# Cross attention scheduled by couples of heads instead of by single units

## The reference, cut to what matters

```python
def cross_attention(h, mem, g_mem, w_cq, w_ckv, w_co):
    q = (h @ w_cq).reshape(n, S, N_HEADS_X, HEAD_DIM_X)        # 4 heads of 128
    k, v = jnp.split(rms_norm(mem, g_mem) @ w_ckv, 2, axis=-1) # 256 memory rows per stream
    s = jnp.einsum('nqhd,nmhd->nhqm', q, k).astype(jnp.float32) * (HEAD_DIM_X ** -0.5)
    p = jax.nn.softmax(s, axis=-1)
    o = jnp.einsum('nhqm,nmhd->nqhd', p, v.astype(jnp.float32)).reshape(n, S, D_X).astype(h.dtype)
    return o @ w_co
```

## Time and profile before

| | |
|---|---|
| median of 3 runs | 2303.09 us (2302.89 to 2307.04) |
| profiled execution, its time | 2302.74 us |
| profiled execution, its span | 2301.0 us |
| PE busy | 2201.2 us, 96% |
| DVE / ACT / POOL busy | 49% / 27% / 34% |
| mean granted TensorE clock | 0.983 |

### The profile page before, as it was taken

How to read it: one execution, slowest core, us unless ns; L and a number is a source line. 1 busy time by engine, 2 the same in 40 slices (tenths; PEclk the granted TensorE clock), 3 DMA queues, 4 the chain that set the end, 5 groups by cost and what they waited for, 6 DMA issues and landing times. The chain is left out here.

```text
span 2301.0 us, 39032 instructions
## 1 busy us (share of the span) xinstructions
PE 2201.2 (96%) x13528; PEld 1931.4 (84%) x13528; DVE 1116.0 (49%) x2157; ACT 627.4 (27%) x1556; POOL 783.1 (34%) x436
## 2 busy tenths in 40 slices
PE   7999999999999999999999999899999999999996
PEld 7988977987788888888798889789878888888885
DVE  3575655537554145235355746554465532551453
ACT  3455454234311011001044554433342110110011
POOL 3311112441344444444331111035323444444442
PEclk9999989999999999999999999899999999999998
DMA  5100121221121121211141001122111221111122
GB/s 216 69 20 22 36 74 39 93 73 37 47 64 64 64 64 64 64 60 58 66 147 38 20 29 38 65 83 74 56 37 56 64 64 62 57 64 64 64 65 82
DMA packets 40286, 145.11 MB, mean 63 GB/s; under 512 B 4688, under 2 KB 4944, under 8 KB 39888
## 3 DMA queue, kind: packets, MB, share of 16 engines
q1 hardware_dynamic: 32832, 117.45, 15.6%
q10 hardware_dynamic: 7312, 25.78, 3.1%
HBM read 133.78 MB, written 9.44 MB: 62 GB/s over the span
## 5 line engine op out<-in xcount | busy, mean ns | idle before, releaser
L742 POOL CAST w_hi<-w_landed_tile 128x1024 fp32r<-128x1024 f32 x216 | 225.1, 1042 | 1469.5 <-PE ps L783 1459.2
L783 PE MATMUL ps<-x_turned,w_hi 128*128 128x512 f32 (+1 forms) x3072 | 666.8, 339 | 3.9 <-DVEq L1352 2.1
L783 PEld LDWEIGHTS ps<-x_turned,w_hi 128*128 128x128 f32 x3072 | 523.1, 188 | 107.5 <-issue 4.3
L744 POOL TENSOR_TENSOR w_lo<-w_landed_tile,w_hi 128x1024 fp32r<-128x1024 f32 x216 | 557.8, 2582 | 17.3
L783 PE MATMUL ps<-w_hi,x_turned 128*128 128x256 f32 (+1 forms) x2304 | 549.4, 321 | 8.1 <-ACT scratch L1209 4.9
L783 PEld LDWEIGHTS ps<-w_hi,x_turned 128*128 128x128 f32 x2304 | 392.6, 194 | 33.0 <-ACT scratch L1209 6.1
L783 PE MATMUL ps<-x_turned,w_lo 128*128 128x512 f32 (+1 forms) x1536 | 394.4, 338 | 0.0
L783 PE MATMUL ps<-w_hi,regions 128*128 128x512 f32 (+1 forms) x1312 | 374.8, 369 | 0.0
L783 PE MATMUL ps<-w_lo,x_turned 128*128 128x256 f32 (+1 forms) x1152 | 360.1, 313 | 0.0
L783 PEld LDWEIGHTS ps<-w_hi,regions 128*128 128x128 f32 x1312 | 238.7, 188 | 42.1 <-DVE x_residual L1465 0.6
L1259 ACT ACTIVATE scratch<-scratch 128x768 f32<-128x768 f32 x44 | 37.3, 848 | 840.3 <-DVE scratch L1522 840.3
(11 more groups left out here) (90 smaller groups left out, 2074.5 us busy)
## 6 DMA issues: line engine op xcount, KB each, us to landing
w_landed_tile<-weights_dram SPq DMA_DIRECT2D x216, 512.0 KB, 3.5
x_hbm<-x_residual ACTq DMA_DIRECT2D x2, 3072.0 KB, 15.3
x_residual<-x_hbm ACTq DMA_DIRECT2D x4, 1536.0 KB, 8.3
rows<-mem_in_dram ACTq DMA_DIRECT2D x8, 512.0 KB, 4.3
scratch<-mem_in_dram ACTq DMA_DIRECT2D x8, 512.0 KB, 5.9
x_residual<-x_in_dram SPq DMA_DIRECT2D x6, 512.0 KB, 5.9
out<-scratch ACTq DMA_DIRECT2D x6, 512.0 KB, 2.7
gain<-gains_dram ACTq DMA_DIRECT2D x3, 512.0 KB, 16.0
```

What stands on the lines that cost most here:

```text
L742: nc.gpsimd.tensor_copy(W_HI[:, s, :], W_IN[:, s, :]).then_inc(w_rounded, 1)
L744: nc.gpsimd.tensor_tensor(W_LO[:, s, :], W_IN[:, s, :], W_HI[:, s, :].bitcast(F32), ALU.subtract).then_inc(w_split, 1)
L783: ins = pe.matmul(dst, lhsT, rhs, start=start, stop=stop, skip_group_check=True)
```

## The change

The stage's items come from `paired_items(("X",))` (line 97), which the other attention stages use already, and `attention_items` is deleted. Step n of `paired_items` holds: both scores of couple n, both softmax items, both `t probs` of couple n-1, gather and normalise of couple n-2, both exps of couple n, side work, both values of couple n-1. There are 14 steps in place of 28. The first 6 steps (before: 11) carry the 13 `crossq` items, the other 8 (before: 17) the 18 items of `t ox` and `coa`. No instruction is added or removed.

```diff
-def attention_items(stage, lag_t=2, lag_pv=3):
...
-    steps = attention_items("X")
+    steps = paired_items(("X",))
     items += flat(q[:2 * KD + AHEAD])
-    items += weave(steps[:2 * NT - 1], q[2 * KD + AHEAD:])
-    items += weave(steps[2 * NT - 1:], [[("t", "ox", t, 0)] for t in range(NT)] + first_heads_out())
+    items += weave(steps[:NT], q[2 * KD + AHEAD:])
+    items += weave(steps[NT:], [[("t", "ox", t, 0)] for t in range(NT)] + first_heads_out())
```

More of the change, by code:

```diff
@@ L119, in paired_items @@
         step += [("value",) + u for u in back]
-        steps.append(step)
-    return steps
-def attention_items(stage, lag_t=2, lag_pv=3):
[L125 to L142, removed]
         steps.append(step)
```

## The result

The changed kernel takes 2321.36 us, median of 6 runs (2317.51 to 2324.66), against 2304.07 for the kernel before (median of 6). The ratio is 1.007, with a 95% interval of 1.0059 to 1.0082: slower by 17.3 us. Its profiled execution took 2320.89 us with a span of 2319.1. The deleted function shifts all later lines by 23: what was line 783 is 760, 835 is 812, 1446 is 1423, 1452 is 1429, 1469 is 1446.

What follows compares the result with a forecast made beforehand. PE, busy 96% of the span, was taken as the bound, so its waits add to the end. A layer: 2.0 + 0 + 5.1 - 1.0 = 6.1 us; two 12.2, clock 3.4, so 15.6 on 2302.74 gives 2318; range 2308 to 2325.

Steps and rivals of the forecast that it cites:

- Part 1: Split of head 2's queries: PE waits 2.83 us instead of 0.84, +2.0 a layer.
- Part 2: Stretch of the output's turnings (t ox), with head 3's split: 5.1 us idle before and after, change 0.
- Part 3: Output projection: five coa wait for the adds, 0.30 + 4.05 + 0.74, in sum 5.1 us a layer.
- Part 4: Fewer changes between kinds: some 5 crossq and 7 coa behind their own kind, -1.0 us a layer.
- Part 5: Clock: one fall to 0.50 in each layer, taken from the new wait of 2.8 us, +1.7 us each.
- (b): Rival: clock falls more often, as waits of 1.3 us come in a row; 2325 us; chance 0.12.
- (a): Rival: waits as forecast, clock holds or even recovers in layer 1; 2313 to 2315 us; chance 0.20.
- (c): Rival: couples fill the t ox stretch; 2305 us, or 2296 to 2298 with adds in time; chance 0.11.
- (d): Rival: the adds alone are in time, saving 8.8 us, the rest as forecast; 2309.5 us; chance 0.12.

Runs made afterwards that it cites:

- ahead4: The changed kernel with one more query projection item ahead of the first score (AHEAD 4 instead of 3); 2314.77 us.
- split_first: The changed kernel with the exps of units 4 and 5 put behind the split of head 2; 2318.73 us.
- coa_pairs: The changed kernel with output projection items given out in whole pairs, both in one step, the last step holding two pairs; 2308.55 us.
- couples_first: The kernel before with couples for the first twelve units only, single units from unit 12 on; 2313.87 us.
- singles_shift: The kernel before (single units) with t ox spread beside projection items and the first output projection item one step earlier; 2308.51 us.

## Why the prediction was right, point by point

The forecast was 2318, with 2308 to 2325 as its range; the median is 2321.36, the rise 17.3 us where 15.6 was worked out. For one layer, 8.7 instead of 6.1 + 1.7 = 7.8. The waits were foreseen one by one; that the total came this near is in part luck, since one term was wrong by 1.0 a layer, another partly made up for it, and the clock's term had the right number for a wrong reason.

- **Part 1**, the split of head 2: right in kind. The wait is 515.07 - (511.36 + 1.13) = 2.6 from place to place, 2.83 forecast. The comparison was mis-sized: I set the whole distance against the 0.84 us that the earlier trace rows give as idle, while from place to place the wait before was 511.99 - 510.89 = 1.1. The rise is 1.5 instead of 2.0, and ahead4 takes 2.6 out. That the exps make ACT late is right, at 0.5 us instead of 0.8 (split_first).
- **Part 2**, the t ox stretch: right. A step takes 544.1 - 540.5 = 3.6 at a clock of 1.00, 3.5 forecast; the stretch grew by 1.8, of which 1.5 is the clock and 0.3 is left. I had called the idle time there an even exchange and it nearly was. The 5.1 idle that I counted before is from place to place; the rows of the timeline mark 2.5 there, and the 3.7 of the earlier trace rows that I quoted for it include 1.4 behind the last coa.
- **Part 3**, the adds: right, and the largest part, as forecast. 560.80 - (558.06 + 1.47) = 1.27 where 1.35 was worked out, three times; 0.8 for the last, 0.4 for the first; 5.0 in all against 5.1, and coa_pairs takes out 4.6 of it, all but the 0.4 of its last step. DVE shows the order that makes it, the multiplication ahead of the adds:

```profile
559.72 0.42 DVE L1423 TENSOR_TENSOR scratch<-scratch,reciprocals 128x256 f32<-128x256 f32 x1
560.07 1.28 DVE L1446 TENSOR_TENSOR x_residual<-ps,x_residual 128x512 f32<-128x512 f32 x2
```

- **Part 4**, fewer changes between kinds: wrong. It was to give 1.0 a layer and gives nothing. A couple's step with two crossq takes 522.40 - 518.21 = 4.19 us, and two single steps took 4.20 (from 508.25 to 510.35, twice). What a crossq saves behind a crossq, and the second score (the 0.07 that I had left to the range), is paid by the two turnings, which take 0.35 (511.01 to 511.36) instead of twice 0.135, and by the two values (0.87 for twice 0.41). On the side of the coa, four of the second items stand behind a wait, and such a one takes 1.50 (554.58 to 556.08), more than the 1.47 behind a turning; in coa_pairs, where they do not wait, 0.5 of the saving comes. This term, 1.0, is more than the whole miss of 0.9 a layer; part 1, worked out 0.4 too dear, parts 2 and 3, 0.3 and 0.2 too cheap, and the clock, 0.2 too dear, nearly cancel.
- **Part 5**, the clock: right in number, one fall a layer in this profile, and nearly in price (1.5 for 1.7), but the reason failed: I took the fall from the long wait for the split of head 2, and the clock stayed at 1.00 behind it in both layers; the falls came behind waits of 1.01 and 0.70, the idle times of rival (b). So the number is luck. The Trainium skill (TensorE: Matmul & The Clock Gate, "Why this matters for your kernels") warns only of gaps longer than any here, and I had read from it that the clock would hold; the traces do not bear that reading out: couples_first shows a fall 1.5 us behind 2.41 us of idle, split_first one behind 1.88, though both show none behind the same wait in the other layer. By windows of 1 us, all five falls inside the stage, over all versions, start 0.1 to 1.5 us behind the end of a wait of PE. Yet ahead4 keeps eight waits a layer and has no fall, and the kernel before none in its stage; whether a given wait will bring one down could not be forecast, and its cause is not shown.
- **Rivals**: (a), a clock that holds in the stage, did not come in this profile, and (b), more than one fall a layer, neither, though the place of the falls is its own; (c), that the couples fill the t ox stretch by themselves, is refuted by its three waits of 0.70 idle. (d), the adds in time, is refuted by the trace, but coa_pairs shows that it would have cost only a different weave. I priced it at 8.8 for both layers, where part 3 itself holds 10.2.

## What to carry to other kernels

Regrouping items in a hand-written order adds no work, so here nearly its whole effect lay in what now stood between a producer and the next user of its buffer: list each such pair, with its latency from start to start, and count what is left between them. Blocks of side work must be given out by the buffer they fill, not by an even count; the waits for the adds here came from pairs that an even count split over two steps, so that the next pair began right behind. Turnings that share the same two banks are no cover for each other; the projection items were.

## What the runs showed of the hardware

A DVE multiplication of two operands in SBUF that started 0.06 us after POOL's subtraction of two SBUF operands took 2.62 us instead of 0.42, and ended 0.28 behind it. With the subtraction moved away (singles_shift) the longest was 0.86. That length, which the kernel before has too, fits the same reading: there the multiplication starts at 513.11 within POOL's rounding of the high part (512.64, 1.04 long) and ends 0.29 behind it. In the changed kernel none in the stage was longer than 0.43. The Trainium skill (SBUF — State Buffer, "SBUF: two separate sides") says that the two engines share a pair of ports that one of them holds for a whole instruction; these rows agree. It makes a schedule's timing on DVE depend on where the next weight tile is prepared, which no list of items shows.

The granted clock is not settled by the order of the work alone: layers of one kernel with the same waits (coa_pairs, split_first, couples_first) differ by 1.5 to 1.6 us in the stage when one has a fall to 0.50 and the other has none. The changed kernel's time scattered over 7 us, and the granted clock goes with it: the two executions with a mean of 0.983 and 0.984 took 2317.5 and 2319.1, the four with 0.981 took 2320.9 to 2324.7. What decides how often the clock falls in an execution was not tested.
